# A two-layer conditioned decoder on eight cores: weights and modulation laid out in one run per partition and piece, later x held back at first, more places for the first convolutions

## The reference, cut to what matters

```
m = silu(c) @ ada_w[layer] + ada_b          # six vectors per layer: shift, scale, gate (mixer, MLP)
h = rmsnorm(x, g) * (1 + sc1) + sh1
layer 0:  p = h @ w_in0                     # 7 x 512 columns: A_b, A_c, A_h, B_q, B_f, B_i, B_g
          y = [A_b * conv3(A_c * A_h),  gated recurrence(q, f, i, g)] @ w_out0
layer 1:  z = gelu(h @ w_in1 + b);  u, v = split(z)
          y = (u * (W_s layernorm(v) + b_s)) @ w_out1
x = x + g1 * y
h = rmsnorm(x, g') * (1 + sc2) + sh2
x = x + g2 * (square(relu(h @ w_ff1)) @ w_ff2)
... and a final rmsnorm
```

## Time and profile before

| | |
|---|---|
| median of 3 runs | 2949.69 us |
| the profiled execution | 2944.09 us |
| its span, first to last instruction, on its slowest core | 2942.6 us |
| spans of its 8 cores | 2907.6 to 2942.6 us |
| matmuls (PE) busy | 2748.9 us, 93% of the span |
| VectorE, ScalarE busy | 1393.9 and 1265.8 us |
| moved by the core's 16 DMA engines | 275.88 MB in 198155 packets |
| weight and modulation pieces | 47 of 1024 KB and 48 of 512 KB at the destination |

### The profile page before, as it was taken

The page is one execution under the profiler, slowest core; times in us unless marked ns, Lnnn a source line. Parts: engine busy times, 40 slices in busy tenths (PEclk is TensorE's granted clock), DMA queues, the critical chain, the costliest instruction groups (busy, mean ns, idle before and its releaser), DMA issues.

```text
span 2942.6 us, 40700 instructions; the slowest of 8 cores (2907.6 to 2942.6 us)
## 1 busy us (share of the span) xinstructions
PE 2748.9 (93%) x13995; PEld 1275.0 (43%) x14271; DVE 1393.9 (47%) x2573; ACT 1265.8 (43%) x2017; POOL 81.5 (3%) x99
## 2 busy tenths in 40 slices
PE   2889999987999999999998899997999999999998
PEld 1444444443444444444443444443444444444443
DVE  1577888875323223233231677763245244244243
ACT  2677888764213223223231677643234234234232
POOL 1000000001000000000001000000000000000000
PEclk9999999999999999999999999997999999999999
DMA  9774444459634043142039575669011011011000
GB/s 176 107 163 129 130 130 130 123 129 163 110 72 86 1 86 74 14 87 61 22 80 154 156 224 170 194 145 217 11 58 50 9 58 43 15 58 37 22 30 29
DMA packets 198155, 275.88 MB, mean 94 GB/s; under 512 B 11456, under 2 KB 93120, under 8 KB 197952
## 3 DMA queue, kind: packets, MB, share of 16 engines
q1 hardware_dynamic: 107344, 198.81, 21.3%
q0 software_dynamic: 90608, 74.45, 18.3%
HBM read 280.56 MB, written 67.11 MB: 118 GB/s over the span
## 4 chain that ended last, share of the span: by engine, by line
PE 80%; DMA 10%; issue 3%; ACT 3%; DVE 3%; SPq 0%; POOL 0%; DVEq 0%; another core or an unknown queue 0%; ACTq 0%; POOLq 0%
PE ps L428 80%; DMA sb_arena<-ada_w 4%; DMA sb_arena<-xs 3%; DMA sb_arena<-x 2%; ACT sb_arena L432 2%; DMA xs<-sb_arena 2%; DVE sb_arena L441 1%; DVE sb_arena L438 1%; ACT sb_arena L434 1%; ACT L338 0%; SPq L452 0%; POOL sb_arena L452 0%; PE ps L717 0%; DVEq L336 0%; DVE sb_arena L685 0%
## 5 line engine op out<-in xcount | busy, mean ns | idle before, releaser
L428 PE MATMUL ps<-sb_arena 128*128 128x512 bf16 (+2 forms) x12915 | 2687.7, 367 | 96.7 <-DVE sb_arena L438 26.7
L428 PEld LDWEIGHTS ps<-sb_arena 128*128 128x128 bf16 (+1 forms) x13185 | 1225.5, 98 | 1527.9 <-issue 154.3
L438 DVE TENSOR_TENSOR sb_arena<-sb_arena 128x512 bf16<-128x512 bf16 (+4 forms) x1224 | 657.1, 549 | 753.8 <-ACT sb_arena L432 711.7
L432 ACT ACTIVATE sb_arena<-ps 128x512 bf16<-128x512 f32 (+1 forms) x705 | 413.2, 596 | 1148.8 <-PE ps L428 1022.2
L441 DVE SCALAR_TENSOR_TENSOR sb_arena<-ps,sb_modc,sb_arena 128x512 f32<-128x512 f32 x384 | 287.3, 750 | 584.0 <-PE ps L428 475.9
L432 ACT ACTIVATE sb_arena<-sb_arena 128x512 f32<-128x512 f32 (+4 forms) x720 | 382.9, 562 | 280.9 <-DVE sb_arena L438 92.9
L434 ACT ACTIVATE sb_arena<-sb_arena,sb_modc,sb_s1c 128x512 bf16<-128x512 f32 x256 | 200.4, 808 | 114.2 <-DVE sb_arena L438 95.1
L338 ACT ACT_TABLE_LOAD x110 | 141.1, 1283 | 2.0
L438 DVE TENSOR_TENSOR sb_arena<-ps,sb_arena 128x512 f32<-128x512 f32 (+1 forms) x128 | 87.3, 683 | 28.9 <-PE ps L428 27.8
L441 DVE SCALAR_TENSOR_TENSOR sb_arena<-sb_arena,sb_vcol 128x512 f32<-128x512 f32 x128 | 90.9, 746 | 14.3 <-ACT sb_arena L432 11.6
L441 DVE SCALAR_TENSOR_TENSOR sb_arena<-sb_arena,ps 128x128 f32<-128x128 f32 x256 | 87.3, 341 | 14.6 <-PE ps L428 7.6
(11 more groups left out here) (39 smaller groups left out, 241.6 us busy)
## 6 DMA issues: line engine op xcount, KB each, us to landing
sb_arena<-xs SPq DMA_DIRECT2D x192, 256.0 KB, 4.4
sb_arena<-x SPq DMA_DIRECT2D x160, 256.0 KB, 4.3
xs<-sb_arena SPq DMA_DIRECT2D x128, 256.0 KB, 4.4
sb_arena<-xs SPq DMA_DIRECT2D x64, 512.0 KB, 5.6
sb_arena<-w_ff POOLq DMA_DIRECT2D x32, 1024.0 KB, 21.3
sb_arena<-ada_w POOLq DMA_DIRECT2D x48, 512.0 KB, 8.4
xs<-sb_arena SPq DMA_DIRECT2D x32, 512.0 KB, 2.9
out<-sb_arena SPq DMA_DIRECT2D x32, 512.0 KB, 2.9
```

The source lines that it names most:

```text
L428: return e.matmul(out, lhsT, rhs, start=start, stop=stop, skip_group_check=skip)
L432: f = lambda e: e.activation(out=out, in_=in_, func=func, scale=scale)
L438: return P.op(q, lambda e: e.tensor_tensor(out=out, in0=in0, in1=in1, op=op), reads, writes, cost)
```

## The change

Each weight and modulation matrix is rearranged on the host, before the kernel, into pieces of [128, n], so that what a partition gets of a piece is one run: 16 KB in memory (8 KB at the destination) for a weight piece, 8 KB (4 KB) for a modulation piece. The bytes, the order of the pieces and their places stay. Every `x_load` gets one more thing to wait for, the second piece of `w_out0` (`xgate`), so that only the x of tiles 0 and 1, which is not loaded by `x_load`, comes before it. For tiles 0 and 1 the convolution has four places for z and for C's projection, by j; the two new ones lie at 88 and 97 KB, over `Sr` and `Sb`. The planner's model gets other rates for the two queues and lets one slow the other. An assertion is added that orders overlapping buffers.

```diff
+    RATE = {"pool": 310e3, "sp": 350e3}
...
                 s = max(dma_free[q], free[q])
-                dma_free[q] = s + o.nbytes / 233e3
+                d = o.nbytes / self.RATE[q]
+                other = max(0.0, dma_free["sp" if q == "pool" else "pool"] - s)
+                dma_free[q] = s + d + 0.7 * min(d, other)
...
-    adaw_d = dt("ada_w", [2, D, 6 * D], F32, kind="ExternalInput").ap()
-    win0_d = dt("w_in0", [D, 3584], F32, kind="ExternalInput").ap()
+    adaw_d = dt("ada_w", [2, 24, 128, 2048], F32, kind="ExternalInput").ap()
+    win0_d = dt("w_in0", [7, 128, 4096], F32, kind="ExternalInput").ap()
...
-            def load_w(k, kind, src):
-                pool_dma(slot_view(k, kind), src, [], [wslot[k]], wds[k], 2 << 20)
+            def load_w(k, src):
+                pool_dma(view(k * SLOT, [128, SLOT // 2], BF16)[0], src, [], [wslot[k]], wds[k], 2 << 20)
...
-                wv = adaw_d[l].rearrange("(kc p) e -> p kc e", p=128)
-                pool_dma(ap, wv[:, :, pc * 256:(pc + 1) * 256], [], [b], ds, 1 << 20)
+                pool_dma(ap.rearrange("p a b -> p (a b)"), adaw_d[l, pc], [], [b], ds, 1 << 20)
...
+            z2, z2b = Region(88 * KB).take("z2", [128, 2, TT + 8], F32, 2)
+            av2, av2b = Region(97 * KB).take("ac2", [128, 2, TT], BF16, 2)
+            zs = [(zz[:, 0, :], zzb[0]), (zz[:, 1, :], zzb[1]), (z2[:, 0, :], z2b[0]), (z2[:, 1, :], z2b[1])]
...
-                dma("sp", xr[:, s, :], src[c, :, t * TT:(t + 1) * TT], sbufs, [xrb[s]], xls[s], 1 << 18)
+                dma("sp", xr[:, s, :], src[c, :, t * TT:(t + 1) * TT], sbufs, [xrb[s]], xls[s], 1 << 18, after=xgate)
...
+                z, zb = zs[j if t < 2 else r]
+                av, avb = avs[j if t < 2 else r]
...
             for k in range(2):
-                load_w(WO0 + k, "k", wo0v[:, :, k * 512:(k + 1) * 512])
+                load_w(WO0 + k, wout0_d[k])
+            xgate.append(wlast[-1])
...
+def pieces(w, n, rows):
+    lead = w.shape[:-2]
+    d, e = w.shape[-2:]
+    if rows:
+        p = w.reshape(lead + (n, d // n // 128, 128, e)).swapaxes(-3, -2)
+    else:
+        p = np.moveaxis(w.reshape(lead + (d // 128, 128, n, e // n)), -2, -4).swapaxes(-3, -2)
+    return np.ascontiguousarray(p.reshape(lead + (n, 128, -1)))
```

More of the change, by code:

```diff
@@ L137, in op @@
                 if x.w is not None:
+                    assert b.w is not None and x.w < b.w, (b.name, x.name)
                     preds.add(x.w)
@@ L354, in build_program @@
     consts_d = dt("consts", [128, NCONST], F32, kind="ExternalInput").ap()
-    adaw_d = dt("ada_w", [2, D, 6 * D], F32, kind="ExternalInput").ap()
-    win0_d = dt("w_in0", [D, 3584], F32, kind="ExternalInput").ap()
[L357 to L361, removed]
+    adaw_d = dt("ada_w", [2, 24, 128, 2048], F32, kind="ExternalInput").ap()
+    win0_d = dt("w_in0", [7, 128, 4096], F32, kind="ExternalInput").ap()
+    wout0_d = dt("w_out0", [2, 128, 4096], F32, kind="ExternalInput").ap()
+    win1_d = dt("w_in1", [4, 128, 4096], F32, kind="ExternalInput").ap()
+    wout1_d = dt("w_out1", [2, 128, 4096], F32, kind="ExternalInput").ap()
+    wff1_d = dt("w_ff1", [2, 8, 128, 4096], F32, kind="ExternalInput").ap()
+    wff2_d = dt("w_ff2", [2, 8, 128, 4096], F32, kind="ExternalInput").ap()
     gmws_d = dt("gm_ws", [4, 128, 128], F32, kind="ExternalInput").ap()
@@ L587, in record @@
             zz, zzb = RM.take("z", [128, 2, TT + 8], F32, 2)
+            z2, z2b = Region(88 * KB).take("z2", [128, 2, TT + 8], F32, 2)
+            av2, av2b = Region(97 * KB).take("ac2", [128, 2, TT], BF16, 2)
+            zs = [(zz[:, 0, :], zzb[0]), (zz[:, 1, :], zzb[1]), (z2[:, 0, :], z2b[0]), (z2[:, 1, :], z2b[1])]
+            avs = [(acv[:, 0, :], acvb[0]), (acv[:, 1, :], acvb[1]), (av2[:, 0, :], av2b[0]), (av2[:, 1, :], av2b[1])]
             RM = Region(186.25 * KB)
@@ L602, in record @@
             nx = {}
+            xgate = []
             def x_load(ring, src, sbufs, c, t):
@@ L790, in m0_conv @@
                 r = j % 2
+                z, zb = zs[j if t < 2 else r]
+                av, avb = avs[j if t < 2 else r]
                 bk = m0_proj(t, WC, j)
[L792 to L796, removed]
+                act(av, ps[:, bk, :], AF.Copy, [bank[bk]], [avb])
+                bk = m0_proj(t, WH, j, [avb])
+                act(z[:, 0:2], hal[:, j, 0:2], AF.Copy, [halb[j]], [zb], 0.22)
+                tt(z[:, 2:TT + 2], ps[:, bk, :], av, ALU.mult, [bank[bk], avb], [zb])
+                act(acc[:, r, :], z[:, 2:TT + 2], AF.Identity, [zb, b_vcol], [accb[r]], 0.75, bias=vc(V_CONVB, j),
                     scale=vc(V_CONVW, 8 + j))
-                act(hal[:, j, 0:2], zz[:, r, TT:TT + 2], AF.Copy, [zzb[r]], [halb[j]], 0.22)
+                act(hal[:, j, 0:2], z[:, TT:TT + 2], AF.Copy, [zb], [halb[j]], 0.22)
                 for tap in (1, 0):
-                    stt(acc[:, r, :], zz[:, r, tap:tap + TT], vc(V_CONVW, tap * 4 + j), acc[:, r, :], ALU.mult, ALU.add,
-                        [zzb[r], accb[r], b_vcol], [accb[r]])
-                bk = m0_proj(t, WB, j, [zzb[r]])
+                    stt(acc[:, r, :], z[:, tap:tap + TT], vc(V_CONVW, tap * 4 + j), acc[:, r, :], ALU.mult, ALU.add,
+                        [zb, accb[r], b_vcol], [accb[r]])
+                bk = m0_proj(t, WB, j, [zb])
                 tt(ycAs[p][:, j, :], ps[:, bk, :], acc[:, r, :], ALU.mult, [bank[bk], accb[r]], [ycAbs[p][j]])
@@ L831, in record @@
             for k, ch in ((WV, 5), (WC, 1), (WH, 2), (WB, 0), (WF, 4), (WG, 6), (WQ, 3)):
-                load_w(k, "k", w0v[:, :, ch * 512:(ch + 1) * 512])
+                load_w(k, win0_d[ch])
             memset(hal[:], 0.0, halb)
@@ L888, in ffn @@
                 w2 = [slot_view(k, "w") for k in m2s]
-                v1 = wff1_d[l].rearrange("(kc p) e -> p kc e", p=128)
-                v2 = wff2_d[l].rearrange("(fc p) d -> p fc d", p=128)
                 ho, xo = (144, 128) if final else (128, 144)
@@ L987, in run @@
                         for i in range(half * 4, half * 4 + 4):
-                            load_w(m1s[i], "k", v1[:, :, i * 512:(i + 1) * 512])
+                            load_w(m1s[i], wff1_d[l, i])
                         for i in range(half * 4, half * 4 + 4):
-                            load_w(m2s[i], "w", v2[:, i * 4:(i + 1) * 4, :])
+                            load_w(m2s[i], wff2_d[l, i])
                     for t in range(NT):
@@ L1157, in run @@
                     for i in (2, 3, 0, 1):
-                        load_w((i + 2) % 4, "k", w1v[:, :, i * 512:(i + 1) * 512])
+                        load_w((i + 2) % 4, win1_d[i])
                     for i in range(2):
-                        load_w(4 + i, "k", wo1v[:, :, i * 512:(i + 1) * 512])
+                        load_w(4 + i, wout1_d[i])
                     for k in range(8):
@@ L1298, in make_in_maps @@
     shared = {
-        "rows": np.ascontiguousarray(rows), "consts": consts, "ada_w": ada_w,
-        "w_in0": f(w_in0)[0], "w_out0": f(w_out0)[0], "w_in1": f(w_in1)[0], "w_out1": f(w_out1)[0],
-        "w_ff1": f(w_ff1), "w_ff2": f(w_ff2), "gm_ws": f(gm_ws)[0],
+        "rows": np.ascontiguousarray(rows), "consts": consts, "ada_w": pieces(ada_w, 24, False),
+        "w_in0": pieces(f(w_in0)[0], 7, False), "w_out0": pieces(f(w_out0)[0], 2, False), "w_in1": pieces(f(w_in1)[0], 4, False), "w_out1": pieces(f(w_out1)[0], 2, False),
+        "w_ff1": pieces(f(w_ff1), 8, False), "w_ff2": pieces(f(w_ff2), 8, True), "gm_ws": f(gm_ws)[0],
     }
```

## The result

The changed kernel took 3061.12 us (median of 4 runs, 3031.4 to 3445.03) where the kernel before took 2950.28 (2945.2 to 2954.17). Over the comparable runs (of the changed kernel 3031.4, 3032.74 and 3038.04 us) the ratio is **1.0285, 95% interval 1.026 to 1.031**: slower by 2.9%, some 84 us. Comparable runs leave out executions in which one die ran at a lower clock; the medians given for this kernel and for experiments 2, 3 and 7 contain some. The profiled execution took 3031.4 us, its span 3029.9: +87.3 us against the span before. Forecast were 2977 us and a range of 2920 to 2996: the direction and the mechanism of the layout held, the size did not.

The account below looks back on a forecast made before the run. Matmuls were 80% of the chain of waits, so only PE's waits for data could move. Start +4, first change +20, third +5, modulation -2 gave +27 on the median 2949.7: 2977 us, range 2920 to 2996.

Parts of the forecast that it names:

- How the engines share: Queues alternate one descriptor each; 8 KB weight descriptors take 700 ns, so x gets 41 GB/s while weights are queued.
- the rival that x keeps its share: Everywhere beside weights: switching by equal packets or cut runs leaves x its share, giving 2925 us; chance 28%.
- The start: Layer 0's beginning: tile 1's x lands at about 82.5 us instead of 78.6, +4 us.
- The bound of +30: Upper end for the start, if an 8 KB descriptor takes 1.2 us.
- First change of phase: Near 709 to 734 us: x load beside six weight pieces ends at 755 instead of 734, +20 us; ends -2, +43.
- Third change: Near 1980 to 2050 us: the first change's pattern, with some weight pieces held back, +5 us; ends -1, +12.
- a standing PE holds back weights and lets x through: Third change: pieces waiting for matmuls to free places reduce the cost from half the first change's price to +5 us.
- Second change: Near 1585 to 1635 us: weights are all queued before x is asked for and drain sooner, 0 us.
- Modulation pieces: Layer 0's feed-forward, six tiles: shorter pieces remove about 2 of 5.3 us of PE waits, -2 us; ends -5, 0.
- Gate and places: Held-back x loads (0, ends 0 and +4) and more places for first convolutions (0, ends -4 and +4 us).
- Planner's rates: New rates for the planner's queues change only the written order, 0 us; ends -5 and +5.
- the order at the gates above stays by its keys: In the planner's order, tile 1's squares stay ahead of the convolutions; part of the 0 us put on rates.

Follow-up runs that it names:

- experiment 2: One-run layout alone on the kernel before, order unchanged, but transfers cut to short descriptors of 512 and 256 elements: 2944.18 us, ratio 0.9978.
- experiment 3: The kernel before with the planner's new rates alone, only the written order changing: 2972.84 us, ratio 1.0091.
- experiment 7: The kernel before with the planner's new rates and its fixed time to landing raised from 2.0 to 4.0 us: 2937.11 us, ratio 0.9952.
- experiment 8: The whole change with old rates, x laid out by tile and partition so two-block transfers have 4 KB descriptors instead of 2 KB: ratio 1.0119.
- experiment 10: The whole change with 4.0 us landing, long weight and modulation descriptors only in the start, x of tiles 0 and 1 in 8 KB descriptors: 2923.03 us.
- experiment 12: The whole change with old rates, weights' descriptors cut from 8 KB to 4 KB: two comparable runs, 2967.79 and 2970.31 us.
- experiment 4: The whole change (layout, held-back x, more places) with the planner's old rates: 2999.96 us, ratio 1.0182 against the kernel before.
- experiment 5: The kernel before with held-back x and four places for the first convolutions alone, old layout and rates: ratio 0.9977.

## Why the prediction was right in kind and wrong in size

*How the engines share.* Right, and near the number: 8 KB takes 666 to 764 ns (700 taken), 4 KB 367 (360 taken), x gets 39 GB/s (41 worked out), counts one to one up to 8 KB. Experiments 2, 8, 10 and 12 vary either side's size and the share follows. The counts don't tell turns of one descriptor from turns of several, equally many on both sides. Of the rule in the Trainium skill (DMA: Bandwidth & Descriptors, SWDGE vs HWDGE vs iDMA) that prefers packets of at most 4096 B as the unit of switching: had two 2 KB descriptors of x gone in one such turn, 72 to 80 us would show two to one; it shows 165 to 163. The rival that x keeps its share fell with it.

*The start: +4 forecast, +19 measured* (table, experiment 4; 10 less than with the layout alone, whose order has no held-back x, but only 5 less by the median of the cores). Two inputs failed. Tile 1's x was issued at 44 us, not 38, and took its turns only from some 48 on (11 packets from 44 to 48 us). And x had weights beside it nearly to its end (squares of the last quarter at 96.4): from 48 to 96 us the DMA view counts 933 packets of weights and modulation, 58 per engine, where the sum had 53. The sum took 8 packets per engine and piece where there are 9, and left out the modulation piece that POOL issues at 71.75 us behind the seven of `w_in0`. That is 58 x 0.785 = 46 us from 48 on, then the rest of x and its landing. The bound of +30 held.

```profile
q0 software_dynamic: 933, 6.19, 74.9%
q1 hardware_dynamic: 1077, 2.07, 17.0%
...
71.75 0.53 POOL L456 DMA_DIRECT2D sb_arena<-ada_w  x1 [7.05 <-DMA sb_arena<-w_in]
```

*First change of phase: +20 forecast, +15 measured* with the old rates (34.3 - 19.2; by the median of the cores 40.7 - 19.1 = 22), +30.5 in the whole change, inside its ends of -2 and +43. This term is right in size too. With the new order the store that starts the pair is itself the late one (30.05 us).

*Third change: +5 forecast, +26 measured* in experiment 4 (58.7 - 32.7), above its end of +12. The step that failed: "a standing PE holds back weights and lets x through". POOL issued eight pieces between 2028 and 2069 us there, as their places came free before PE stood or with its last matmuls, so none was held back, and PE then waited 38.46 us at once (34.8 to 38.7 on the eight cores; before, at most 6.8). The lines are PE's before, then PE's and the last two pieces in experiment 4:

```profile
2009.45 16.56 PE L428 MATMUL ps<-sb_arena 128*128 128x512 bf16 x63 [6.78 <-DVE sb_arena L438]
2030.96 9.15 PE L428 MATMUL ps<-sb_arena 128*128 128x512 bf16 x31 [4.94 <-ACT sb_arena L434]
```
```profile
2096.70 43.58 PE L430 MATMUL ps<-sb_arena 128*128 128x512 bf16 x191 [38.46 <-ACT sb_arena L436]
...
2060.36 0.53 POOL L454 DMA_DIRECT2D sb_arena<-w_ff  x1 [0.99 <-DMA sb_arena<-w_ff]
2068.55 0.53 POOL L454 DMA_DIRECT2D sb_arena<-w_ff  x1 [7.66 <-DMA sb_arena<-w_ff]
```

Even the full count, half the first change's price or +10, was too low. From 2041 to 2097 us the DMA view counts 985 packets of weights (62 per engine, 48 us at 0.785) and 1837 of x (115), to which loads of 512 KB for the feed-forward belong; the first change had been counted with 48 and 71.

*Second change: 0 forecast.* PE waits 23.79 us for `gm_ws`, which the prediction didn't look at: a small transfer on x's queue starves as well. Layer 1's mixer takes most of it up: +4 net over both with the old rates (32.7 - 28.6).

*Modulation pieces: -2 forecast*, -5.7 in experiment 4 (28.6 - 34.3), just past its end of -5, but -1.6 by the median of the cores (39.1 - 40.7); PE's waits for them fall from 5.3 to 0.2 us. With the new order PE's waits for them are 5.6 us, as in the earlier trace rows, and nothing is gained.

*Gate and places: 0 forecast*, and no loss in experiment 5.

*Planner's rates: 0 within 5 forecast, +27 measured* (experiment 3). This is the second step that failed: "change only the order that is written; the order at the gates above stays by its keys". The gates did stay, but the steady tiles, in which PE had been dense, went from 72.3 to 76.9 us; they weren't looked at, since PE hardly waited there before (1.5 us in all from 420 to 580 us; 8.0 with the rates alone). Of the missing 57 us (84 against 27) this is 27, the third change some 21, the start 15; the first change gives 5 back, all read on the slowest cores. Without the rates the time would have been 2999.96 us, still above the range of 2996.

What stays open: the whole change's first change of phase costs 15 us more than with the old rates although layout and rates alone would add to +14 there (15.6 and -1.4), and by the median of the cores 34.5 against 22; which of the reordered stores does that was not isolated.

## What to carry to other kernels

Where two queues share the engines descriptor by descriptor, the size of the other queue's descriptors sets your share: lengthening one side cost 54 us here, and lengthening both in the start gave the same time as lengthening neither. Look for every small transfer (residual blocks, tables) that the next phase waits for. A gain in transfer efficiency (q0's time fell by a fifth) is worth nothing where PE waits for the other queue. A planner's rate and its time to landing are one model: changing the first alone made the order worse by 27 us, changing both made it better by 14. And a stretch without waits is no reason to put a new order at nothing: the steady tiles had next to none before.

## What the runs showed of the hardware that was not expected

Sharing one to one holds at every pair of sizes seen, 2 KB beside 8 KB (163 to 165), 4 KB beside 8 KB (130 to 129) and 8 KB beside 8 KB (118 to 118), and where loads and stores stand together on x's queue (507 to 512 from 2085 to 2110 us of the changed kernel). A store of 256 KB that lands in 4.7 us at the median of the whole span took 43 us there. TensorE's granted clock was lower where PE waited: from 737 to 800 us of the changed kernel, with PE busy for 26 of 63 us, its mean was 0.70 of the upper level of 2.4 GHz, so part of it at the lower of 1.2; in the dense stretch from 800 to 850 it was 0.97. From 640 to 850 us that makes 0.85, before 0.94.
